# Streaming 1088 tokens past each weight tile as 512, 512 and 64 columns instead of 364, 364 and 360

## What is computed

```python
h = _rmsnorm(x, norm_ffn1) * (1 + sc1) + sh1
x = x + 0.5 * g1 * _swiglu(h, w1_gate, w1_up, w1_down)
u = _rmsnorm(x, norm_mix) * (1 + sc2) + sh2
p = u @ w_in + b_in
ca, cg, q, k, v, o, ga, gb, ip, fp = _split_cols(p)
glu = ca * jax.nn.sigmoid(cg)
y, conv_new = _causal_dwconv(glu, conv_buf, w_dw, b_dw)          # 31 taps
a_out = jax.nn.silu(_layernorm(y, ln_conv_g, ln_conv_b)) @ w_conv_out
hm, C, n, m = _mlstm_chunkwise(heads(q), heads(k), heads(v), ip, jax.nn.log_sigmoid(fp), C0, n0, m0, chunk)
hm = _headnorm(hm, mh_norm).reshape(Bn, T, D_MLSTM).astype(x.dtype)
b_out = (jax.nn.sigmoid(o) * hm) @ w_mlstm_out
z = jax.nn.sigmoid(ga) * a_out + jax.nn.sigmoid(gb) * b_out
x = x + g2 * (z @ w_out)
h = _rmsnorm(x, norm_ffn2) * (1 + sc3) + sh3
x = x + 0.5 * g3 * _swiglu(h, w2_gate, w2_up, w2_down)
```

## Time and profile before

| what | before |
|---|---|
| time, median of 2 runs | 3420.56 us (3418.02 and 3423.1) |
| span of the profiled execution | 3417.0 us, 1.0 and 6.1 us below the two runs |
| PE busy | 3167.0 us (93%) |
| PEld busy | 3029.7 us (89%) |
| DVE busy | 1597.9 us (47%) |
| POOL busy | 1020.0 us (30%) |
| ACT busy | 465.6 us (14%) |
| granted clock, mean | 0.957 |

### The profile page before, as it was taken

How to read it: one execution, slowest core, us unless ns; L and a number is a source line. 1 busy time by engine, 2 the same in 40 slices (tenths; PEclk the granted TensorE clock), 3 DMA queues, 4 the chain that set the end, 5 groups by cost and what they waited for, 6 DMA issues and landing times.

```text
span 3417.0 us, 47244 instructions
## 1 busy us (share of the span) xinstructions
PE 3167.0 (93%) x18860; PEld 3029.7 (89%) x18860; DVE 1597.9 (47%) x2811; ACT 465.6 (14%) x746; POOL 1020.0 (30%) x449
## 2 busy tenths in 40 slices
PE   8999999999968889879888997989998999999995
PEld 8999999999958778878787895789887999999995
DVE  5122233222276943973694397476344233232335
ACT  2000000000031122012112211322012000000001
POOL 1233333333312311321231142034332333333331
PEclk9999999999989999999999998999998999999997
DMA  6312121212121112212211221222210111111111
GB/s 221 106 62 74 61 74 61 74 61 68 49 75 41 44 42 68 70 34 60 74 50 42 68 70 51 60 103 93 108 50 25 44 44 44 47 43 43 43 43 59
DMA packets 83136, 217.63 MB, mean 64 GB/s; under 512 B 28352, under 2 KB 28480, under 8 KB 82496
## 3 DMA queue, kind: packets, MB, share of 16 engines
q1 hardware_dynamic: 83000, 215.86, 19.7%
q10 hardware_dynamic: 8, 0.00, 0.0%
HBM read 184.03 MB, written 31.81 MB: 63 GB/s over the span
## 4 chain that ended last, share of the span: by engine, by line
PE 73%; DVE 16%; issue 5%; DVEq 3%; POOL 1%; DMA 1%; ACT 1%; SPq 0%; ACTq 0%; POOLq 0%
PE slots L575 61%; DVE y L1072 12%; PE bank_x L637 3%; PE bank_x L758 2%; DVEq L1376 2%; PE bank_x L750 1%; PE bank_x L765 1%; PE bank_y L762 1%; PE bank_y L767 1%; DVE work L1100 1%; PE bank_y L637 1%; DMA w_raw<-w_units_dram 1%; PE bank_y L740 1%; PE bank_x L775 0%; PE bank_x L748 0%
## 5 line engine op out<-in xcount | busy, mean ns | idle before, releaser
L543 POOL TENSOR_TENSOR w_hi<-w_raw,one 128x1024 fp32r<-128x1024 f32 x220 | 437.9, 1990 | 2317.9 <-PE slots L575 2247.3
L575 PE MATMUL slots<-u_hi,w_hi 128*128 128x364 f32 (+1 forms) x4032 | 930.3, 339 | 53.0 <-DVE u_lo L1133 20.2
L575 PE MATMUL slots<-u_hi,w_lo 128*128 128x364 f32 (+1 forms) x4032 | 899.5, 332 | 0.0
L575 PE MATMUL slots<-u_lo,w_hi 128*128 128x364 f32 (+1 forms) x4032 | 898.4, 331 | 0.0
L575 PEld LDWEIGHTS slots<-u_hi,w_hi 128*128 128x128 f32 x4032 | 699.4, 191 | 81.4 <-issue 65.4
L575 PEld LDWEIGHTS slots<-u_hi,w_lo 128*128 128x128 f32 x4032 | 705.3, 190 | 9.2 <-issue 8.7
L575 PEld LDWEIGHTS slots<-u_lo,w_hi 128*128 128x128 f32 x4032 | 708.2, 191 | 0.0
L545 POOL TENSOR_TENSOR w_lo<-w_raw,w_hi 128x1024 fp32r<-128x1024 f32 x220 | 581.3, 2642 | 17.2
L1163 DVE TENSOR_TENSOR work<-work,slots 128x1092 f32<-128x1092 f32 x44 | 56.9, 1292 | 913.5 <-PE slots L575 913.5
L1072 DVE SCALAR_TENSOR_TENSOR y<-glu,dw_cur,y 128x1024 f32 (+1 forms) x240 | 344.7, 1436 | 9.1
L1072 DVE SCALAR_TENSOR_TENSOR x<-slots,m_g,x 128x728 f32<-128x728 f32 x368 | 257.8, 742 | 0.0
(11 more groups left out here) (219 smaller groups left out, 2187.4 us busy)
## 6 DMA issues: line engine op xcount, KB each, us to landing
w_raw<-w_units_dram SPq DMA_DIRECT2D x220, 512.0 KB, 3.6
ada<-ada_units_dram SPq DMA_DIRECT2D x72, 512.0 KB, 4.2
st<-state_dram SPq DMA_DIRECT2D x32, 257.0 KB, 3.7
C_s_out<-st SPq DMA_DIRECT2D x32, 257.0 KB, 3.6
x_keep<-x SPq DMA_DIRECT2D x1, 4368.0 KB, 12.7
ga_keep<-th SPq DMA_DIRECT2D x8, 546.0 KB, 5.6
gb_keep<-th SPq DMA_DIRECT2D x8, 546.0 KB, 5.6
th<-gb_keep SPq DMA_DIRECT2D x8, 546.0 KB, 4.6
```

Of the source, the lines that this page charges most:

```text
L543: pool.tensor_tensor(w_hi[:, slot, :], w_raw[:, slot, :], one[:].to_broadcast([P, D]), ALU.mult).then_inc(w_hi_done, 1)
L575: last = pe.matmul(slots[:, s, g, 0:b - a], w_of(w), r[:, k, a:b], start=(k == 0 and q == 0), stop=(k == K - 1 and q == 2))
```

## The change

`GROUPS` becomes (0, 512), (512, 1024), (1024, 1088). The three groups of a result then follow each other in PSUM without a gap, and `bank3` is one run of 1092 words, the last four of which no matmul writes. `tile3` goes. The prompt's 1024 words are now exactly the first two banks, so that `residual` and `conv_value` read them in one operation where there were two, and the samples lie at the start of the third bank. `W` stays 1092. Left out below are the other readers, which change in the same way as the one of `gate`.

```diff
-GW = 364
-GROUPS = [(0, GW), (GW, 2 * GW), (2 * GW, NT)]
-W = 3 * GW
-LP = NP - 2 * GW
+BANK = 512
+GROUPS = [(0, BANK), (BANK, NP), (NP, NT)]
+W = NT + 4
...
         def bank3(s):
 
-            return slots[:, s, :, 0:GW]
-
-        def tile3(ap):
-            return ap.rearrange("p (g n) -> p g n", g=3)
+            return slots[:, s].rearrange("p g n -> p (g n)")[:, 0:W]
...
                 def gate():
                     s, done, _ = jobs.take_unit()
                     act.wait_ge(unit_done, done)
-                    act.activation(tile3(sg), bank3(s), ACT.Silu).then_inc(slot_free[s], 1)
+                    act.activation(sg, bank3(s), ACT.Silu).then_inc(slot_free[s], 1)
...
                 g = m_g[:, p, m, :]
-                dve.tensor_tensor(sample3(xs_tmp[:]), sample3(slots[:, s, 2, LP:LP + NB * TB]), per_batch(g[:, 1:NV]), ALU.mult)
-                x01 = x[:, m, 0:2 * GW].rearrange("p (g n) -> p g n", g=2)
-                stt(x01, slots[:, s, 0:2, 0:GW], g[:, 0:1], x01, ALU.mult, ALU.add)
-                stt(x[:, m, 2 * GW:NP], slots[:, s, 2, 0:LP], g[:, 0:1], x[:, m, 2 * GW:NP],
-                    ALU.mult, ALU.add).then_inc(slot_free[s], 1)
+                dve.tensor_tensor(sample3(xs_tmp[:]), sample3(slots[:, s, 2, 0:NB * TB]), per_batch(g[:, 1:NV]), ALU.mult)
+                xp = x[:, m, 0:NP]
+                stt(xp, bank3(s)[:, 0:NP], g[:, 0:1], xp, ALU.mult, ALU.add).then_inc(slot_free[s], 1)
                 dve.drain()
...
                 b = bias_of(h1, 9 + 2 * t)
-                stt(glu[:, t, PAST:PAST + 2 * GW].rearrange("p (g n) -> p g n", g=2), slots[:, s, 0:2, 0:GW], b,
-                    th[:, t, 0:2 * GW].rearrange("p (g n) -> p g n", g=2), ALU.add, ALU.mult)
-                stt(glu[:, t, PAST + 2 * GW:PAST + NP], slots[:, s, 2, 0:LP], b, th[:, t, 2 * GW:NP], ALU.add, ALU.mult)
-                stt(glus[:, t, :, PAST:PAST + TB], sample3(slots[:, s, 2, LP:LP + NB * TB]), b,
+                stt(glu[:, t, PAST:PAST + NP], bank3(s)[:, 0:NP], b, th[:, t, 0:NP], ALU.add, ALU.mult)
+                stt(glus[:, t, :, PAST:PAST + TB], sample3(slots[:, s, 2, 0:NB * TB]), b,
                     sample3(th[:, t, NP:NT]), ALU.add, ALU.mult).then_inc(slot_free[s], 1)
```

More of the change, by code:

```diff
@@ L865, in root @@
                 act.wait_ge(part_done, done)
-                act.activation(tile3(dst), bank3(s), ACT.Sqrt, bias=eps[:, 0:1]).then_inc(slot_free[s], 1)
+                act.activation(dst, bank3(s), ACT.Sqrt, bias=eps[:, 0:1]).then_inc(slot_free[s], 1)
             def norm(p):
@@ L917, in _ @@
             act.wait_ge(rows_dve, 1)
-            act.activation(tile3(rows[0:4, ROW_I, :]), slots[0:4, s, :, 0:GW], ACT.Identity, bias=b_if[0:4, 0:1])
-            act.activation(tile3(rows[0:4, ROW_Z, :]), slots[32:36, s, :, 0:GW], ACT.Identity,
+            act.activation((rows[0:4, ROW_I, :]), bank3(s)[0:4], ACT.Identity, bias=b_if[0:4, 0:1])
+            act.activation((rows[0:4, ROW_Z, :]), bank3(s)[32:36], ACT.Identity,
                            bias=b_if[32:36, 0:1]).then_inc(slot_free[s], 1)
@@ L932, in gate_tile @@
                 act.wait_ge(unit_done, done)
-                act.activation(tile3(n), bank3(s), ACT.Tanh, bias=bias, scale=0.5).then_inc(slot_free[s], 1)
+                act.activation(n, bank3(s), ACT.Tanh, bias=bias, scale=0.5).then_inc(slot_free[s], 1)
             def rows_to_exp():
@@ L967, in section_a @@
                     act.wait_ge(unit_done, done)
-                    act.activation(tile3(qkvo[:, j, :]), bank3(s), ACT.Identity, bias=bias_of(h, j),
+                    act.activation((qkvo[:, j, :]), bank3(s), ACT.Identity, bias=bias_of(h, j),
                                    scale=HD ** -0.5 if j < 2 else 1.0).then_inc(slot_free[s], 1)
@@ L1162, in product @@
                     dve.wait_ge(unit_done, done)
-                    dve.tensor_tensor(tile3(prod), tile3(sg), bank3(s), ALU.mult).then_inc(slot_free[s], 1)
+                    dve.tensor_tensor(prod, (sg), bank3(s), ALU.mult).then_inc(slot_free[s], 1)
                     prods.add()
@@ L1511, in gated @@
                 if n < KT:
-                    stt(tile3(z[:, m, :]), tile3(th[:, n % 2, :]), 1.0, bank3(s), ALU.add, ALU.mult).then_inc(slot_free[s], 1)
+                    stt((z[:, m, :]), (th[:, n % 2, :]), 1.0, bank3(s), ALU.add, ALU.mult).then_inc(slot_free[s], 1)
                 else:
                     dve.drain()
-                    stt(tile3(th[:, n % 2, :]), tile3(th[:, n % 2, :]), 1.0, bank3(s), ALU.add, ALU.mult).then_inc(slot_free[s], 1)
+                    stt((th[:, n % 2, :]), (th[:, n % 2, :]), 1.0, bank3(s), ALU.add, ALU.mult).then_inc(slot_free[s], 1)
                     dve.drain()
@@ L1522, in _ @@
             dve.wait_ge(part_done, done)
-            dve.tensor_copy(tile3(ysum), bank3(s)).then_inc(slot_free[s], 1)
+            dve.tensor_copy(ysum, bank3(s)).then_inc(slot_free[s], 1)
             dve.drain()
```

## The result

The changed kernel takes 3740.63 us (median of 2 runs, 3740.13 and 3741.13) against 3420.56 before: a ratio of 1.0938, 95% interval 1.0917 to 1.0958. The forecast was 3757 us. Its profiled execution has a span of 3739.3 us, 322.3 more than before.

A forecast was written before the change was run, and what follows sets the result against it. TensorE's pace was taken as the bound, except where VectorE's convolution taps end last. Span 3417 us plus 342 for about 4390 slower passes, less 5 of corrections, gave 3754, so a forecast time of 3757 us; range 3609 to 3809.

The forecast's parts named there:

- The load behind C: After C, a pass's 64-column matmul, the next pass's weight load stands exposed: 111 to 115 ns to its first matmul.
- the rival of two loads ahead: Two loads run ahead during a 512-column matmul, so the short matmul hides its load: no change, 3420 us; chance 0.10.
- that of columns alone: Matmuls cost only columns and a small constant: a pass of 457 ns, 40 shorter, time 3245 us; chance 0.04.
- The rival of a load that waits for its predecessor's end: The next load begins only after the 64-column matmul streams off, 138 ns in all: some 3867 us; chance 0.03.
- the rival in which the 14.5 ns vanish: The 14.5 ns a matmul above streaming vanish with longer matmuls: 215 ns for 512 columns, 3609 to 3625 us; chance 0.08.
- the middle of the bounds: 512-column matmuls take 228 ns (fixed cost) to 234 (slower rate); a pass of three matmuls was taken as 575 ns.
- The hidden passes: In four heads' projections, 820 passes, 78 ns longer each, cost nothing: TensorE's waits for `ap_h` take them up.
- correction (a): In a head's pieces, waits for other engines' answers take up part of the slower passes: 6.5 us off (0 to 13).
- the rival of the falling clock: Gaps at the 64-column matmul halve the FFN's granted clock: 5300 us, or 3910 with a tenth of passes; chance 0.03.
- correction (b): After long waits, at half clock, a pass becomes 1067 ns; ten such entries of six passes add 5 us.
- (c): Where waits for `ap_h` shrink from 17 to a few us, the clock may stay up: 4 us off (0 to 8).
- the straight line: VectorE's residual, one instruction of 1024 columns for two, extrapolated to 1.28 us, 0.2 less; 37 us in all, off the path.

The follow-up runs named there:

- narrow weights: The changed kernel with each weight tile cut to its first 64 columns, token columns still 512, 512, 64: 3509.88 us.
- four splits: The changed kernel with token columns 448, 512, 128; 384, 512, 192; 352, 512, 224; 288, 512, 288: 3625.32, 3507.38, 3451.56, 3421.12 us.
- balanced split: The changed kernel with the accumulator begun 224 words into its first bank, columns 288, 512, 288: 3421.12 us, 1.0003 of the kernel before.
- doubled short matmul: The changed kernel with the 64-column matmul of each pass done twice: 4365.63 us.

## Why the prediction was right

**The load behind C**, the step on which the forecast rested, holds: the trace after shows the load starting with C, narrow weights take two thirds of the loss away, and four splits follow it within 0.2%. With that the rival of two loads ahead falls (no load starts before C), and so does that of columns alone. The rival of a load that waits for its predecessor's end would have had C at 138 ns, where it is 110.

**The 512-column matmuls** took 232 ns; the rival in which the 14.5 ns vanish needed 215. That the middle of the bounds came out was luck, as nothing had spoken for it. The balanced split shows what lies behind it: its pass of 497 ns less 232 leaves 132.5 for each matmul of 288 columns, so (232 - 132.5)/224 = 0.444 ns a column, and only 4 or 5 ns a matmul. The 364 columns of before fit: 162 + 4 to 5, against 165.6.

**The hidden passes.** The projections of the four heads grew by 0.3, 0.8, 1.8 and 0 us, read from the end of one named wait to the next. At 77 ns for each of 820 passes they would have grown by 63. The conversion of TensorE's waits into work is shown by the waits view and, once they were used up, by the doubled short matmul.

**What was mis-sized.** The sum had 337 us for 322. Split at the same waits, the FFNs with their ends took 242 us more, where 3168 passes at 78 ns are 247; the pieces, from the waits for `ap_h` to those for `hs_p` (L1410), 10.4, 11.1, 10.0 and 3.1 us, 34.7 in all; the stretch behind them up to the second FFN 42.7, where 576 passes at 78 ns are 45; and the stretch ahead of the first FFN 3. The term that failed is correction (a). Among the pieces lie 619 passes; at 77 ns they are 48 us, of which 13 did not come, the upper bound of (a) and not the 6.5 I took. Nor is it in the main what (a) says, a wait that takes up slower passes. The last matmul ahead of a piece, before and after, with the piece's first one after:

```profile
1277.64 0.32 PE L575 MATMUL slots<-u_hi,w_lo 128*128 128x360 f32 x1
...
1404.25 0.19 PE L571 MATMUL slots<-u_hi,w_lo 128*128 128x64 f32 x1
1404.37 0.23 PE L736 MATMUL bank_y<-qkvo 128*8 128x8 f32 x3
```

Before, the piece follows at 1277.89, after 0.25 us and not the 0.16 of 360 columns; now it follows after 0.12 and not the 0.03 of 64. The 0.09 us behind the pass were there before, so that no new load is exposed and this pass gets no longer. Of the 240 places where a piece follows 119 are like this, 9 of the 13 us. At 16 others the time grew by over 0.1 us less than 77 ns a pass would have it, as with the wait at 1261.90; they hold 6 us, and the rest give 2 back.

The stage of the gates and of the first convolution tiles, for which I had hidden passes and no gain, became 3.6 us shorter. That is luck: in VectorE's chain ahead of `glus` two operations on four partitions took 1.90 and 3.35 us before (L1297, L1299) and take 0.21 and 1.21 now (L1291, L1293). The change does not touch them, and in the balanced split they take 1.90 and 3.35 again; why they vary is open.

The clock in the FFN stayed at 1.00 as forecast; that the rival of the falling clock is no idle one shows in the doubled short matmul, at 688 ns a pass. At the lower level a pass takes 1.06 us (from 2779.13 to 2780.19, at a granted clock of 0.50), as correction (b) had it; (c) cannot be told apart from the rest.

**Off the path**, the residual came down to 1276 ns, as the straight line had it, 38 us of VectorE's time in all, and the time did not move with it: its cover held.

## What to carry to other kernels

Where each matmul loads its weights anew, look at the shortest matmul of a loop and not at the mean: it costs the load behind it, and columns given to it from its neighbours are free until it is as long as that load (112 ns here; some 240 columns, an estimate from the 6 to 7 ns that were still missing at 224). A cheaper way to read an accumulator is worth nothing if its price is such a split, and the two can be had apart: an offset in the first bank kept the one run of words and the balanced split. A wait that hides added work should be stated with its length, since 1.3 us were left of 17.4.

## What the runs showed of the hardware

The granted clock can fall in a stage that never waits for another engine: with two exposed loads a pass and runs of sixteen 9-column matmuls its mean was 0.97 in the first FFN; with the same runs and one exposed load it was 1.00, and so it was with two and no such runs. The float32r matmuls of 288, 364 and 512 columns take 0.444 ns a column and 4 to 5 ns more each, where the rows of the plain f32 ones followed two clocks a column within 1 ns. The load of a piece's weights did not run ahead at the two places shown: it began 0.25 us behind the start of a 360-column matmul and 0.12 behind that of a 64-column one.
